# Eight of the 48 conditioning units of a two-layer decoder trunk: reduced on VectorE in a transposed layout instead of by GpSimd, ScalarE and TensorE

## The reference, cut to what matters

```python
cond = jax.nn.silu(c)
for l in range(DEPTH):                                   # DEPTH = 2
    mod = cond @ w_ada[l] + b_ada[l]                     # (1024) @ (1024, 6144)
    sh1, sc1, g1, sh2, sc2, g2 = [m[:, None, :] for m in jnp.split(mod, 6, axis=-1)]
    h = _rms_norm(x, norm1_gain[l]) * (1.0 + sc1) + sh1
    ...                                                  # projections, four head groups, o
    x = x + g1 * (o @ w_out[l])
    h = _rms_norm(x, norm2_gain[l]) * (1.0 + sc2) + sh2
    x = x + g2 * _conv_glu_ffn(h, w_ffn_up[l], ffn_conv_w[l], ffn_conv_b[l], w_ffn_down[l])
return _rms_norm(x, final_gain)
```

## Time and profile before

| | |
|---|---|
| median of 3 runs | 736.09 us (735.74 to 736.74) |
| profiled execution, first to last instruction | 734.9 us; about 1.2 us of the measured time lies outside it |
| TensorE matmul busy | 708.8 us, 96% |
| VectorE busy | 502.5 us, 68% |
| ScalarE busy | 408.9 us, 56% |
| GpSimd busy | 128.7 us, 18% |
| DMA | 159.32 MB, mean 217 GB/s |

### The profile page before, as it was taken

The page is one execution under the profiler, slowest core; times in us unless marked ns, Lnnn a source line. Parts: engine busy times, 40 slices in busy tenths (PEclk is TensorE's granted clock), DMA queues, the critical chain, the costliest instruction groups (busy, mean ns, idle before and its releaser), DMA issues.

```text
span 734.9 us, 13705 instructions
## 1 busy us (share of the span) xinstructions
PE 708.8 (96%) x5581; PEld 642.3 (87%) x5581; DVE 502.5 (68%) x905; ACT 408.9 (56%) x664; POOL 128.7 (18%) x96
## 2 busy tenths in 40 slices
PE   6999999999999999999999999989999999999995
PEld 4688777788999999999998987878989999999994
DVE  2365787645699797887767368964569666667666
ACT  3257755644565565656445765674457445554452
POOL 2000104104005535555100010320400000000002
PEclk9999999999999999999999999999999999999998
DMA  9979999565187868686934776466516566555511
GB/s 308 363 195 259 372 351 324 196 229 172 59 274 243 271 196 293 210 261 222 342 121 139 260 256 229 161 240 220 181 60 229 138 208 236 195 199 172 175 55 57
DMA packets 120673, 159.32 MB, mean 217 GB/s; under 512 B 6035, under 2 KB 93220, under 8 KB 120612
## 3 DMA queue, kind: packets, MB, share of 16 engines
q1 hardware_dynamic: 120612, 158.46, 65.9%
HBM read 156.81 MB, written 1.64 MB: 216 GB/s over the span
## 4 chain that ended last, share of the span: by engine, by line
PE 81%; ACT 6%; DVE 6%; issue 3%; DMA 2%; SPq 1%; POOL 0%; DVEq 0%; POOLq 0%; ACTq 0%
PE bank L983 23%; PE bank L984 22%; PE bank L985 22%; PE bank L995 4%; ACT work L1610 2%; DMA direct<-in_w_ada 2%; ACT w_hi L1455 2%; DVE w_lo L1728 1%; PE bank L1314 1%; PE bank L1035 1%; PE bank L1011 1%; PE bank L1345 1%; PE bank L1204 1%; SPq L754 1%; PE bank L1202 1%
## 5 line engine op out<-in xcount | busy, mean ns | idle before, releaser
L1728 DVE TENSOR_TENSOR w_lo<-raw,w_hi 128x2048 fp32r<-128x2048 f32 (+1 forms) x97 | 233.4, 2406 | 99.1 <-ACT w_hi L1455 99.1
L983 PE MATMUL bank<-act_hi,w_hi 128*128 128x256 f32 (+1 forms) x1024 | 293.6, 287 | 1.4 <-DVE work L2020 0.8
L985 PE MATMUL bank<-act_hi,w_lo 128*128 128x256 f32 (+1 forms) x1024 | 289.7, 283 | 0.0
L984 PE MATMUL bank<-act_lo,w_hi 128*128 128x256 f32 (+1 forms) x1024 | 289.6, 283 | 0.0
L1455 ACT ACTIVATE w_hi<-raw 128x2048 fp32r<-128x2048 f32 (+1 forms) x97 | 183.0, 1887 | 134.3 <-PE bank L985 131.5
L983 PEld LDWEIGHTS bank<-act_hi,w_hi 128*128 128x128 f32 (+1 forms) x1024 | 195.5, 191 | 16.1 <-issue 13.2
L984 PEld LDWEIGHTS bank<-act_lo,w_hi 128*128 128x128 f32 (+1 forms) x1024 | 195.6, 191 | 0.4
L985 PEld LDWEIGHTS bank<-act_hi,w_lo 128*128 128x128 f32 (+1 forms) x1024 | 195.5, 191 | 0.0
L2020 DVE SCALAR_TENSOR_TENSOR work<-bank,vec,work 128x254 f32<-128x254 f32 (+1 forms) x176 | 76.5, 476 | 10.1 <-ACT work L1670 8.6
L983 PE MATMUL bank<-mlp_hi,w_hi 128*128 128x256 f32 x192 | 54.7, 285 | 0.0
L984 PE MATMUL bank<-mlp_lo,w_hi 128*128 128x256 f32 x192 | 54.3, 283 | 0.0
(11 more groups left out here) (217 smaller groups left out, 978.2 us busy)
## 6 DMA issues: line engine op xcount, KB each, us to landing
direct<-in_w_ada SPq DMA_DIRECT2D x48, 1024.0 KB, 9.6
raw<-in_w_ffn_up SPq DMA_DIRECT2D x44, 1024.0 KB, 5.2
raw<-in_w_in SPq DMA_DIRECT2D x22, 1024.0 KB, 6.3
raw<-in_w_ffn_down SPq DMA_DIRECT2D x22, 1024.0 KB, 5.0
raw<-in_w_out SPq DMA_DIRECT2D x8, 1024.0 KB, 6.3
bias<-toeplitz SPq DMA_DIRECT2D x4, 384.0 KB, 11.2
heads_out<-in_x SPq DMA_DIRECT2D x1, 1024.0 KB, 5.1
out<-heads_out SPq DMA_DIRECT2D x4, 256.0 KB, 2.2
```

The costliest lines, as they stand in the source:

```text
L983: pe.matmul(dst, lh, rh, start=first, stop=False, skip_group_check=check)
L984: pe.matmul(dst, lh, rl, start=False, stop=False, skip_group_check=check)
L985: return pe.matmul(dst, ll, rh, start=False, stop=last, skip_group_check=check)
L1728: nc.vector.tensor_tensor(w_lo[n % RAW][:, s], raw[n % RAW][:, s], w_hi[n % RAW][:, s].bitcast(F32), ALU.subtract).then_inc(lo_done, 1)
```

## The change

The eight units of the second layer come in another layout. The host adds an input `ada_rows`: for each unit and each of its two blocks of 128 features, one feature per partition, with its 1024 weights along the row. Silu(c) is needed once, on all partitions: SyncE loads `c` broadcast to 128 partitions into `cond_row` (the query and key buffer of the first head group, free once the layer's probabilities have met the values), and ScalarE applies silu to it in step 0 of the MLP. VectorE then forms each feature by one `tensor_tensor_reduce` over 1024 elements, two for a unit (`sum_unit`), one unit in each of the steps 3 to 10, between `taps(j, 0)` and the `split_lo` behind it. GpSimd's multiplications and sums, ScalarE's `ada_scale`, TensorE's `ada_columns` and VectorE's `take_columns` go; one bias addition for all 16 columns comes after step 10. The loads stand in SyncE's queue where they stood; `wait_used` still waits on `ada_summed`, which VectorE now raises.

```diff
--- before.py
+++ after.py
...
@@ -435,6 +434,7 @@
         ki_twice = work[:, 1664:1920].rearrange("p (t a d) -> p t a d", t=TT, a=2)
         latn = work[:, 1152:1664].rearrange("p (t w d) -> p t w d", t=TT, w=2)
         lf_wide = v_sb[:, 1:3, :, :].rearrange("p g t n -> p (g t n)").rearrange("p (c q) -> p c q", c=TT * HEADS)
+        cond_row = qkT[:, 0, :, :, :].rearrange("p a b t -> p (a b t)")
         conv = work[:, 0:1024].rearrange("p (w f t) -> p w f t", w=2, f=2)
         silu = work[:, 1024:1536].rearrange("p (f t) -> p f t", f=2)
         prod = work[:, 1536:2048].rearrange("p (f t) -> p f t", f=2)
...
@@ -729,9 +726,7 @@
                                  w_ada[l].rearrange("(k p) n -> p k n", p=P)[:, 4 * half:4 * half + 4, c0:c0 + 2 * UC]).then_inc(
                         direct_in[a % DSLOTS], 16)
                 elif kind == "ada":
-                    sp.dma_start(slot[:, :].rearrange("p (k n) -> p k n", k=KT),
-                                 w_ada[l].rearrange("(k p) n -> p k n", p=P)[:, :, u * UC:(u + 1) * UC]).then_inc(
-                        direct_in[a % DSLOTS], 16)
+                    sp.dma_start(slot[:, :], ada_rows_in[u]).then_inc(direct_in[a % DSLOTS], 16)
                 else:
                     sp.dma_start(slot[:, 0:256], w_dq_up[l]).then_inc(direct_in[a % DSLOTS], 16)
                     sp.dma_start(slot[:, 256:512], w_didx_q[l]).then_inc(direct_in[a % DSLOTS], 16)
@@ -823,6 +818,9 @@
                             load_bias()
                 for e in gap_units(2 * l + 1):
                     load_direct(direct_at[e])
+                if l + 1 < DEPTH:
+                    sp.wait_ge(pv_ready, NV * (l + 1))
+                    sp.dma_start(cond_row, c[0].partition_broadcast(P)).then_inc(cond_in, 16)
                 load_mlp(l, 0, "gate", 0)
                 load_mlp(l, 1, "value", 0)
                 for j in range(STEPS - 1):
@@ -867,31 +865,6 @@
                                     pattern=[[-1, P]], channel_multiplier=1)
             nc.gpsimd.affine_select(out=upto[:, :], in_=upto[:, :], compare_op=ALU.is_ge, fill=0.0, base=0,
                                     pattern=[[1, SEQ]], channel_multiplier=-1).then_inc(consts, 1)
-            def ada_sum(l, u):
-
-
-                a, n = direct_at[("ada", l, u)], sum_no[(l, u)]
-                w = direct[a % DSLOTS]
-                if (l, u) in scaled_no:
-                    pool.wait_ge(ada_scaled, scaled_no[(l, u)] + 1)
-                else:
-                    pool.wait_ge(direct_in[a % DSLOTS], direct_value(a))
-                    nc.gpsimd.tensor_tensor(w[:, :].rearrange("p (k n) -> p k n", k=KT),
-                                            w[:, :].rearrange("p (k n) -> p k n", k=KT),
-                                            cond[:, :, 0:1].to_broadcast([P, KT, UC]), ALU.mult).then_inc(pool_scaled, 1)
-                    pool.wait_ge(pool_scaled, multiplied_no[(l, u)] + 1)
-                for step in range(1, 3):
-                    if step > 1:
-
-                        pool.wait_ge(ada_added, 2 * n + step - 1)
-                    m = KT * UC >> step
-                    nc.gpsimd.tensor_tensor(w[:, 0:m], w[:, 0:m], w[:, m:2 * m], ALU.add).then_inc(ada_added, 1)
-                pool.wait_ge(ada_added, 2 * n + 2)
-
-                pool.wait_ge(ada_turned, ada_no(l, u) - 1)
-                half = slice((u % 2) * UC, (u % 2 + 1) * UC)
-                nc.gpsimd.tensor_tensor(ada_row[:, half], w[:, 0:UC], w[:, UC:2 * UC], ALU.add).then_inc(ada_summed, 1)
-
             def inverse_root(n):
 
                 pool.wait_ge(ms_inv, n + 1)
@@ -961,9 +934,6 @@
                                                     ALU.add).then_inc(own_ready, 1)
                 sum_squares(2 * l + 1)
                 inverse_root(2 * l + 1)
-                for j in range(STEPS):
-                    for e in mlp_ada(l, j):
-                        ada_sum(e[1], e[2])
             pool.wait_ge(gain_in, 16)
             for q in range(2):
                 pool.wait_ge(x_out, q + 1)
@@ -1010,17 +980,6 @@
                 for ct in range(4):
                     mm = pe.transpose(pair_bank(l, u)[:, ct * P:(ct + 1) * P], ada_row[:, ct * P:(ct + 1) * P], ident[:, :])
                 mm.then_inc(ada_turned, 2)
-
-            def ada_columns(l, u, n):
-
-
-                pe.wait_ge(mod_ready, ada_no(l, u))
-                pe.wait_ge(ada_summed, sum_no[(l, u)] + n)
-                for ct in range(2 * n):
-                    c0 = (u % 2) * UC + ct * P
-                    mm = pe.matmul(bank[7][:, ct:ct + 1], ada_row[:, c0:c0 + P], ones[:, 0:1], start=True, stop=True)
-                mm.then_inc(ada_turned, n)
-                turned[0] = ada_no(l, u + n)
 
             turned = [SETUP_ADA]
 
@@ -1440,8 +1399,6 @@
                         turn_x(j - 2)
                     up(j, 1)
                     down(j - 1)
-                    for e in mlp_ada(l, j - LAG)[:1]:
-                        ada_columns(e[1], e[2], 2)
                 down(STEPS - 1)
 
 
@@ -1469,18 +1426,8 @@
                 for unit in pair_units(l, u):
                     wait_used(act, direct_at[("ada", l, unit)])
 
-                act.wait_ge(ada_turned, ada_no(l, u))
+                act.wait_ge(ada_turned, 2 * pair_no[(l, u)])
                 nc.scalar.activation(ada_row[:, :], pair_bank(l, u)[:, :], ACT.Copy).then_inc(ada_rows, 1)
-
-            def ada_scale(l, u):
-
-                a = direct_at[("ada", l, u)]
-                w = direct[a % DSLOTS]
-                act.wait_ge(direct_in[a % DSLOTS], direct_value(a))
-                for k in range(KT):
-                    ins = nc.scalar.activation(w[:, k * UC:(k + 1) * UC], w[:, k * UC:(k + 1) * UC], ACT.Identity,
-                                               scale=cond[:, k, 0:1])
-                ins.then_inc(ada_scaled, 1)
 
             def modulated(n, l, shift, k0=0, k1=KT):
 
@@ -1677,6 +1624,9 @@
                     last_tap(j, 0)
                     if j == 0:
                         take_rows(*GAP_PAIRS[2 * l + 1][1])
+                        if l + 1 < DEPTH:
+                            act.wait_ge(cond_in, 16)
+                            nc.scalar.activation(cond_row, cond_row, ACT.Silu).then_inc(cond_spread, 1)
                     split_hi(first + (3 * j + 3 if j < STEPS - 1 else 3 * STEPS - 1))
                     last_tap(j, 1)
                     act.wait_ge(conv_read, 2 * (STEPS * l + j) + 1)
@@ -1688,9 +1638,6 @@
 
                         act.wait_ge(unit_used, first + 3 * j + 2)
                     nc.scalar.activation(gated(j)[0], prod, ACT.Copy).then_inc(mlp_hi_ready, 1)
-                    for e in mlp_ada(l, j):
-                        if e[1:] in scaled_no:
-                            ada_scale(e[1], e[2])
                     if l + 1 == DEPTH and 1 <= j < 5:
 
                         g = j - 1
@@ -1764,7 +1711,7 @@
             def take_mod(l, u):
 
                 n = ada_no(l, u + 2)
-                dve.wait_ge(ada_turned, n)
+                dve.wait_ge(ada_turned, 2 * pair_no[(l, u)] + 2)
                 c0 = 2 * pair_units(l, u)[0]
                 s = slice(c0, c0 + 4)
                 nc.vector.tensor_reduce(mod[:, l, s], pair_bank(l, u)[:, :].rearrange("p (c g r) -> p c g r", g=4, r=32)[:, :, :, 0],
@@ -1780,11 +1727,15 @@
                                                    vec[:, 0, V_N1 + 4 * c:V_N1 + 4 * c + 4], ALU.add, ALU.mult))
                 modulated(0, 0, 0, 4 * c, 4 * c + 4)
 
-            def take_columns(l, u, n):
-
-                dve.wait_ge(ada_turned, ada_no(l, u + n))
-                nc.vector.tensor_tensor(mod[:, l, 2 * u:2 * (u + n)], bank[7][:, 0:2 * n],
-                                        vec[:, l, V_BADA + 2 * u:V_BADA + 2 * (u + n)], ALU.add).then_inc(mod_ready, n)
+            def sum_unit(l, u):
+
+                a = direct_at[("ada", l, u)]
+                dve.wait_ge(direct_in[a % DSLOTS], direct_value(a))
+                for f in range(2):
+                    w = direct[a % DSLOTS][:, f * D_MODEL:(f + 1) * D_MODEL]
+                    ins = nc.vector.tensor_tensor_reduce(w, w, cond_row, 1.0, 0.0, ALU.mult, ALU.add,
+                                                         mod[:, l, 2 * u + f:2 * u + f + 1])
+                ins.then_inc(ada_summed, 1)
 
             def wait_mod(n):
 
@@ -2033,8 +1984,10 @@
                     taps(j, 0)
                     if j < 2:
                         take_mod(*GAP_PAIRS[2 * l + 1][j])
-                    for e in mlp_ada(l, j - LAG - 1)[:1]:
-                        take_columns(e[1], e[2], 2)
+                    if l + 1 < DEPTH and j == 2:
+                        dve.wait_ge(cond_spread, 1)
+                    for e in mlp_ada(l, j - 1)[:1] + mlp_ada(l, j - 2)[1:]:
+                        sum_unit(e[1], e[2])
                     split_lo(first + (3 * j + 3 if j < STEPS - 1 else 3 * STEPS - 1))
                     taps(j, 1)
```

(19 more changed lines are left out.)

## The result

The kernel after takes 749.19 us (median of 4 runs, 748.95 to 749.56), the kernel before 736.41 in the same rounds (735.74 to 736.93): ratio 1.0168 [1.0153, 1.0183], 12.8 us or 1.7% slower. The forecast was 746.8 with a range of 742.0 to 750.5.

What follows compares the result with a forecast made beforehand. The prediction took TensorE, busy 96% of the span, as the bound. Its terms, -3.6 (column blocks) + 2.3 (silu) + 10.2 (queue) + 1.8 (clock) = +10.7 us, gave 746.8 us, range 742.0 to 750.5.

Steps and rivals of the forecast that it cites:

- TensorE's four blocks, -3.6: First MLP: four `ada_columns` blocks go, 0.89 us each; TensorE gets all of it, 3.6 us saved.
- GpSimd and ScalarE, nothing: First MLP: `ada_sum` and `ada_scale` lie behind work already waiting for TensorE, so losing them brings nothing.
- VectorE's sums: MLP steps 3 to 9: two operations of 1.22 us make 2.4 us a unit, covered, cost nothing.
- The rival of a VectorE that becomes the bound: Steps 3 to 10 slip if a sum takes 4.6 us or its unit is late: 749 to 756, chance 0.12.
- `cond_row` in the queue, nothing: SyncE before the first gate unit: its load goes out near 159.1 us, landing with 4 us to spare; no cost.
- Silu, 2.3: Step 0 on ScalarE: table load 1.28 us plus silu 1.06, together 2.3 us, all on TensorE's path.
- the rival that charges 1.4 us more: Step 0: the table switch also drains ScalarE, costing 1.4 us more, 748.2 us; chance 0.05.
- The queue, 10.2: Step 10: the last down unit's load waits behind the gap unit for VectorE's last sum; TensorE waits 10.2 us.
- The clock, 1.8: Behind the wait before `down(10)`: TensorE restarts at 1.2 GHz instead of 2.4, losing 1.8 us.
- Ahead of the MLP, nothing: Stretch before the first MLP: the forecast's sum holds no term for it.
- The rival on the other side: TensorE's saved blocks decide if SyncE passes the last gap unit by about 358: 734.8 or 732.5 us, chance 0.05.

Runs made afterwards that it cites:

- the fast version: Kernel after, with silu before the second take_rows and the last down unit and second layer's first two units loaded ahead of the gap units: 732.93 us.
- the filled waits: Kernel after, with unread matmuls in TensorE's two waits of the first MLP: 754.05 us with 20 and 78, 745.39 us with 10 and 38.
- the down unit first: Kernel after, with the load of the last down unit moved ahead of the four gap units in SyncE's queue: 744.02 us.
- three loads first: Kernel after, with the last down unit and the second layer's first two units loaded ahead of the four gap units: 737.41 us.
- paired sums: Kernel after, with VectorE summing both units of a load pair in one step, the last in step 9, SyncE's order unchanged: 737.16 us.
- silu alone: Kernel before, with only the load of cond_row and silu behind the second take_rows added, its result unread: 739.09 us, ratio 1.0042.
- the doubled kernel: Kernel after with silu early and three loads ahead of the gap units, plus a second unread copy of each VectorE sum: 736.79 us.

## Why the prediction was right, point by point

- **TensorE's four blocks, -3.6.** Right: 0.89 at each, and 3.9 (2.7 to 4.6) in the fast version, where nothing else is left.
- **GpSimd and ScalarE, nothing.** Right: 72 us less on GpSimd and 12.5 on ScalarE, and no run shows a gain beyond TensorE's own blocks.
- **VectorE's sums.** Forecast 1.22 us each; 16 of 1.217 us came. Hidden in steps 3 to 9, shown up to double the cost. The rival of a VectorE that becomes the bound falls.
- **`cond_row` in the queue, nothing.** Right: the first gate unit goes out at 159.37 (forecast 159.1) and ScalarE is not kept waiting.
- **Silu, 2.3.** Measured 2.4. A drain of ScalarE is not seen: silu starts 1.30 us after the table load does, as forecast, so the rival that charges 1.4 us more falls here.
- **The queue, 10.2.** Measured 10.1. Each link came: sum of the last unit to 370.10 (forecast 368.2; the half clock of step 0 and the 0.4 of scatter ahead of the MLP are the difference), 0.44 to the issue, 7.5 to landing, then the split. Undoing it from either end gives the term back.
- **The clock, 1.8.** Right in kind and too small. Behind the long wait it cost 1.6. The mis-sized term is this one: I costed the clock only for the wait of 10 us and not for the 2.8 us in step 0, which cost another 1.5. That the 1.8 came so near to 1.6 is partly luck: it was the difference between 16 transposes at 0.23 us and 40 at 0.12, and the 40 are no transposes (see the filled waits). Transposes do start 0.11 us apart at full clock, (0.60 - 0.27) / 3 in the four of the earlier trace rows, 0.27 being the length of one; but the profile shows a granted clock of 1.00 in the opening too, and no run shows that the clock is what makes the first 16 slow.
- **Ahead of the MLP, nothing.** Right: the 0.4 us at 195 us lie within the scatter of that point.

So +12.4 instead of +10.7: 1.5 of clock and 0.4 of scatter ahead of the MLP, less small errors. The rival on the other side, in which the saved blocks decide, named the condition (the down unit must pass the last gap unit) that the fast version then met.

## What to carry to other kernels

When the last reader of a ring's buffer moves to another engine, ask when the buffer now comes free, and then what is queued behind the load that waits for it: here a sum that ended 18 us later held back an unrelated unit that its own engine needed next, and then, with that unit moved, the ones behind. Small work on an engine that is not the bound is free in the middle of a pipeline (here up to 4.9 us a step) while at its end 2.4 us just fitted and all beyond was paid in full; place it by the slack of the step and not by the engine's share. For every wait of TensorE of a few microseconds, add the half-clock stretch that may come behind it, and also for a wait that your remedy leaves or makes.

## What the runs showed of the hardware that I had not expected

**A short wait can cost half clock, and late.** The same wait of 2.77 us in step 0 was followed by some 3 us at 1.2 GHz in the profiles of the kernel after, of those with the down unit first and with three loads first and of the one with paired sums, and not in that with silu alone. The fall came from 0.3 us ahead of the restart (paired sums) to 1.3 us behind it (kernel after), there with TensorE busy. In the doubled kernel a wait of 2.4 us had a half clock behind it, and in the opening one of 1.99 us did and others of 1.38 to 1.93 us did not. What decides it is open; in step 0 it was worth 1.5 us.

**VectorE and GpSimd hold each other up.** VectorE's operations with two inputs in SBUF stretched beside GpSimd's multiplications and additions in the kernel before, and no longer do. VectorE's and GpSimd's timelines in the kernel before, from 219 us:

```profile
220.93 4.12 DVE L2046 TENSOR_TENSOR mlp_lo<-work,mlp_hi 128x512 fp32r<-128x512 f32 x1
224.97 4.48 DVE L1728 TENSOR_TENSOR w_lo<-raw,w_hi 128x2048 fp32r<-128x2048 f32 x1
```

```profile
219.06 5.45 POOL L879 TENSOR_TENSOR direct<-direct,cond 128x2048 f32<-128x2048 f32 x1 [35.51 <-DMA direct<-in_w_ada]
224.58 6.03 POOL L888 TENSOR_TENSOR direct<-direct 128x1024 f32<-128x1024 f32 x2
```

The first stands beside the multiplication, the second beside the additions; alone they take 0.69 and 2.29 us. The other direction stands above: in the kernel with the down unit first, two additions of GpSimd took 3.46 us beside VectorE's subtraction, 1.47 in the kernel before. The groups of these two operations (busy us and mean ns behind the first bar), of the kernel before and then of the kernel after:

```profile
L1728 DVE TENSOR_TENSOR w_lo<-raw,w_hi 128x2048 fp32r<-128x2048 f32 (+1 forms) x97 | 233.4, 2406 | 99.1 <-ACT w_hi L1455 99.1
L2046 DVE TENSOR_TENSOR mlp_lo<-work,mlp_hi 128x512 fp32r<-128x512 f32 x20 | 26.2, 1309 | 0.0
```

```profile
L1675 DVE TENSOR_TENSOR w_lo<-raw,w_hi 128x2048 fp32r<-128x2048 f32 (+1 forms) x97 | 219.1, 2258 | 121.4 <-ACT w_hi L1412 121.3
L1999 DVE TENSOR_TENSOR mlp_lo<-work,mlp_hi 128x512 fp32r<-128x512 f32 x20 | 13.7, 684 | 0.0
```

That is 26.8 us less, more than the 18.9 us of the sums, and it is why VectorE's busy time fell with more work on it; under cover, it was worth nothing. The Trainium skill (SBUF — State Buffer, Who interferes with whom) names this pair, and the trace agrees.

**Matmul and transpose.** A float32 matmul of 128 by 128 took 0.23 us and left two records; transposes of the same size started 0.11 us apart and left one.
